# First FFN's rows by token halves, products ahead of lower parts, later turns, last attention values inside a projection

## The chip, the cores and the metric

One core of a Trainium2 chip runs the whole program. The metric is the device time of one execution in microseconds, the median of several runs. Engines are named as in the profile: PE is TensorE (matmul), PEld its weight loads, DVE is VectorE, ACT is ScalarE, POOL is GpSimd, SP is SyncE, whose queue issues the weight loads from HBM.

## The reference: what is computed

Batch 1, 256 tokens, width 1024, everything in float32. Three layers in a row, each a mixer and a SwiGLU FFN of inner width 2816:

```python
# layer 1 (adaLN: shift, scale, gate come from c)
h = rms_norm(x, norm1_w) * (1 + scale1) + shift1
x = x + gate1 * (concat[gated_delta_rule(h), sliding_window_attention(h)] @ w_out)
h2 = rms_norm(x, norm2_w) * (1 + scale2) + shift2
x = x + gate2 * ((silu(h2 @ w_gate) * (h2 @ w_up)) @ w_down)
# layer 2: short convolution mixer, then FFN
x = x + short_conv_mixer(rms_norm(x, mix_norm[0]));  x = x + swiglu(rms_norm(x, ffn_norm[0]))
# layer 3: dilated attention (3 branches, 16 heads), then FFN
x = x + dilated_attention_mixer(rms_norm(x, mix_norm[1]));  x = x + swiglu(rms_norm(x, ffn_norm[1]))
return rms_norm(x, final_norm)
```

## The kernel before

**Split arithmetic.** Each float32 factor is split into a high part (rounded to the matmul format, fp32r, by a ScalarE copy) and a low part (VectorE: the value less its high part). Each product is three matmuls: high x high, high x low, low x high. Weights come as blocks of 128 x 2048 floats (1 MB) through a ring of three buffers `raw`. For each block SP issues the load when the low part of the block three loads earlier is done (`load`), ScalarE makes `w_hi` (`hi(w)`, L663), VectorE `w_lo` (`lo(w)`, L1049). Both engines go through hand-written queues, strictly in order. `lo_ready`, `block_used` and so on are semaphores; PE's `block_used` tells ScalarE when a weight slot is free.

**An FFN** (`ffn(f)`, f = 0, 1, 2 in each engine's part) has 11 steps j. For each j PE makes gate and up of 256 inner features for token half t = 0 and t = 1 (`gate_up(f, j, t)`, 24 matmuls of 512 columns each into bank B[t]; lhs is the activation, 128 tokens of it). ScalarE takes silu of the gate half (`silu`, L901), VectorE multiplies it with the up half (`product(f, j, t)`, L1512 for f = 0, L1509 else) into `hid`. `turn_hid` turns `hid` with four PE transposes (L2254); ScalarE copies the high part (L906), VectorE makes the low part (L1517). `token_rows` multiplies it with the down block of the step before, in four pieces (feature half c, token half t) of six matmuls each, and `turn_hid(f, j)` stands in the middle of it (`halfway`). For f = 0 and j = 2 to 5 VectorE also has an `accumulate` (L1071 to L1075), two instructions of 1024 columns that build gate2.

**The norm ahead of the first FFN** (norm 1, x kept by features: 8 tiles k of 128 features x 256 tokens). PE spreads the root over the partitions (`rstd`), VectorE scales tile k (L1121), ScalarE makes its high part with the shift added (`h_high`, L688), VectorE the low part (L1126); VectorE's order is scaled(0), scaled(1), low(0), scaled(2), low(1), ... Each is one instruction of 256 columns. `gate_up(0, 0, 0)` waits for the low part of each k. Behind `h_high(1)` ScalarE has the `w_hi` of block 1's gate and up, an activation table load and `silu(0, 0, 0)`; behind `h_parts_2` VectorE has the two `w_lo` and `product(0, 0, 0)`. `gate_up(0, 1, 0)` waits for both `w_lo` and for that product.

**Norms 2 to 5** (x kept by tokens in `xt`) begin inside the last `token_rows` of the layer before. VectorE adds each finished piece to `xt` (`add_piece`, L1480; two instructions, L1477 and L1478, for norm 2). Ahead of the fourth piece (`before_last`) PE turns the first feature half of `xt` (`turn(n, 0)`, 8 transposes, L1769), ScalarE makes the high parts (L925) and squares the pieces (L917), VectorE the low parts (`low(k)`, L1487). PE's next block uses them at once; `turn(n, 1)` comes after its first two k (three for norm 2). VectorE puts the fourth addition behind three low parts for norm 2 and behind four for the others (`ahead`).

**The last attention pair** (a = 5): PE has `scores`, two blocks of the output projection (`ATT_OUT`, `ATT_OUT + 1`), `transposes` (L2033), then `values` (24 small matmuls), which wait for ScalarE's copies of the turned probabilities (L815), and then the blocks `ATT_OUT + 2` and `+ 3`. ScalarE's copies stand behind two `w_hi` of the next FFN. `ATT_OUT + 3` waits for the low part of those values (`pv_lo`).

Of the kernel before, what the change touches and what calls it, by code (L numbers as in the profile page):

```python
# [9 lines left out]
P = 128  # L10
T = 256
TT = T // P
HALF = P // 2
D = 1024
KD = D // P
# [152 lines left out]
class Semaphores:  # L168


    def __init__(self, new):
# [50 lines left out]
        self.t_ready = new("t_ready")  # L222
        self.h_hi_ready = new("h_hi_ready")
# [92 lines left out]
def build(nc, stream, x_in, consts_in, vectors_in, gab_in, t5_onehot, t5_log, rel_bias, out):  # L316
    t5_scratch = nc.dram_tensor("t5_scratch", (16, 384), F32, kind="Internal")
    with ExitStack() as ctx:
# [323 lines left out]
        def _(act):  # L642
# [41 lines left out]
            def h_high(n, ks=range(KD)):  # L684
                for k in ks:
                    act.wait_ge(s.t_ready, 8 * n + k + 1)
                    if n:
                        act.activation(normed(n)[0][:, k, :], nt[:, k, :], ACT.Identity, bias=shift2[:, k:k + 1]).then_inc(s.h_hi_ready, 1)  # L688
                    else:
                        act.activation(normed(n)[0][:, k, :], nt[:, k, :], ACT.Copy).then_inc(s.h_hi_ready, 1)  # L690
# [241 lines left out]
            def ffn(f, following):  # L932
# [3 lines left out]
                else:  # L936
                    squares(1)
                    root(1)
                    h_high(1)
# [98 lines left out]
        def _(dve):  # L1038
# [76 lines left out]
            def h_parts_2():  # L1115
                dve.wait_ge(s.rstd_ready, 2)
                dve.wait_ge(s.mod_ready, 6)
                rstd = B[3][:, 256:512]

                def scaled(k):  # L1120
                    dve.scalar_tensor_tensor(out=nt[:, k, :], in0=x[:, k, :], scalar=a2[:, k:k + 1],  # L1121
                                             in1=rstd, op0=ALU.mult, op1=ALU.mult).then_inc(s.t_ready, 1)

                def low(k):
                    dve.wait_ge(s.h_hi_ready, 8 + k + 1)
                    dve.scalar_tensor_tensor(out=normed(1)[1][:, k, :], in0=nt[:, k, :], scalar=shift2[:, k:k + 1],  # L1126
                                             in1=normed(1)[0][:, k, :], op0=ALU.add, op1=ALU.subtract).then_inc(s.h_lo_ready, 1)

                for k in range(KD):
                    scaled(k)  # L1130
                    if k >= 1:
                        low(k - 1)
                low(KD - 1)
# [348 lines left out]
            def turn(n, last):  # L1482
# [9 lines left out]
                ahead = 3 if n == 2 else 4  # L1492
# [27 lines left out]
            def ffn(f, following):  # L1520
# [6 lines left out]
                for j in range(JF):  # L1527
# [9 lines left out]
                    if j == 1:  # L1537
                        hid_low(f, 0)
                    if 0 < j < JF - 1:
# [3 lines left out]
                    product(f, j, 1)  # L1543
# [123 lines left out]
        def _(pe):  # L1667
# [75 lines left out]
            def token_rows(w, oh_, ol_, k0, banks, order=BY_FEATURES, first=False, r=None, halfway=None, before_last=None):  # L1743
# [758 lines left out]
```

## Time and profile before

| | us |
|---|---|
| median of 3 runs (1001.93, 1002.17, 1003.58) | 1002.17 |
| the profiled execution | 1002.46 |
| its span, first to last instruction | 1000.7 |

| engine | busy us | share |
|---|---|---|
| PE | 972.4 | 97% |
| PEld | 840.5 | 84% |
| DVE | 611.5 | 61% |
| ACT | 476.4 | 48% |
| POOL | 36.8 | 4% |

The profile is of one execution. A row of the timeline is one instruction, or several of the same kind in a row (x4) with their common length; instructions of one engine overlap in their records, so an engine's pace is read from start to start. What stands in brackets is the idle time ahead of the row and the instruction that ended it.

### The profile page before, as it was taken

Reading aid. Unit: us, or ns where it says so; the run is one execution under the profiler, and the core shown is the slowest. Engines: PE = TensorE matmul, PEld = TensorE weight load, DVE = VectorE, ACT = ScalarE, POOL = GpSimd, SP = SyncE. Lnnn points to the kernel's source line nnn. Section 1 sums busy time; section 2 is a strip of 40 time slices with the busy share of each in tenths; the row PEclk is TensorE's granted clock in tenths of the full one; section 3 lists DMA queues with packets and bytes.
Section 4 is the critical chain, followed back from the end, with each engine's and each line's share of the span. In section 5 each row is a group of like instructions: output and inputs, shape, how many; then the busy total and the mean of one; then the engine's idle time right before and its main releaser. Section 6 shows DMA issues by size and latency. Waiting matters only on the chain.

```text
span 1000.7 us, 15257 instructions
## 1 busy us (share of the span) xinstructions
PE 972.4 (97%) x6523; PEld 840.5 (84%) x6523; DVE 611.5 (61%) x751; ACT 476.4 (48%) x635; POOL 36.8 (4%) x37
## 2 busy tenths in 40 slices
PE   5899999999999999999999999999999999999998
PEld 3699988988878888899888888888999888888886
DVE  2478998865656444777764545456776654545444
ACT  3376358446334344634363535355645563535343
POOL 0000542000000000000000000000000000000000
PEclk9799999999999999999999999999999999999999
DMA  9746422866675536364635454544643425464621
GB/s 344 292 155 226 169 86 86 295 236 228 237 267 206 215 131 230 132 224 163 235 115 202 165 214 159 220 151 151 246 167 129 150 103 211 158 220 151 227 85 42
DMA packets 31554, 185.66 MB, mean 186 GB/s; under 512 B 3008, under 2 KB 5504, under 8 KB 10752
## 3 DMA queue, kind: packets, MB, share of 16 engines
q1 hardware_dynamic: 29952, 180.37, 49.9%
q0 software_dynamic: 832, 3.17, 1.0%
q8 instruction: 51, 0.84, 0.3%
q10 hardware_dynamic: 704, 1.17, 0.3%
q14 instruction: 15, 0.12, 0.0%
HBM read 183.62 MB, written 1.07 MB: 185 GB/s over the span
## 4 chain that ended last, share of the span: by engine, by line
PE 80%; DVE 9%; DMA 4%; ACT 4%; issue 2%; POOL 0%; SPq 0%; DVEq 0%; ACTq 0%
PE bank L1669 43%; PE acc L1669 34%; ACT w_hi L663 2%; DVE w_lo L1049 2%; DMA raw<-stream 2%; DMA keys_queries<-stream 2%; PE bank L2254 2%; DVE XT L1210 1%; DMA AT<-stream 1%; DVE soft L1361 1%; DVE keys_queries L1066 0%; DVE XT L1341 0%; PE bank L2033 0%; DVE h_parts L1487 0%; PE bank L1769 0%
## 5 line engine op out<-in xcount | busy, mean ns | idle before, releaser
L1049 DVE TENSOR_TENSOR w_lo<-raw,w_hi 128x2048 fp32r<-128x2048 f32 x145 | 329.3, 2289 | 156.0 <-ACT w_hi L663 155.6
L1669 PE MATMUL bank<-w_hi,h_parts 128*128 128x512 f32 x1056 | 333.5, 391 | 1.3 <-DVE h_parts L1126 1.3
L663 ACT ACTIVATE w_hi<-raw 128x2048 fp32r<-128x2048 f32 x145 | 273.0, 1907 | 100.4 <-PE acc L1669 71.2
L1669 PEld LDWEIGHTS bank<-w_hi,h_parts 128*128 128x128 f32 x1056 | 198.2, 188 | 44.4 <-issue 2.1
L1669 PE MATMUL bank<-w_lo,h_parts 128*128 128x512 f32 x528 | 205.5, 389 | 0.0
L1669 PE MATMUL acc<-h_parts,w_hi 128*128 128x256 f32 x928 | 172.8, 288 | 3.5 <-DVE h_parts L1101 2.5
L1669 PEld LDWEIGHTS acc<-h_parts,w_hi 128*128 128x128 f32 x928 | 145.1, 192 | 7.1 <-issue 5.3
L1669 PE MATMUL acc<-h_parts,w_lo 128*128 128x256 f32 x464 | 132.3, 285 | 0.0
L1669 PE MATMUL acc<-w_hi,o_hi 128*128 128x512 f32 x296 | 118.9, 402 | 0.0
L1669 PEld LDWEIGHTS bank<-w_lo,h_parts 128*128 128x128 f32 x528 | 99.2, 188 | 19.9
L1669 PE MATMUL acc<-w_hi,o_lo 128*128 128x512 f32 x296 | 115.6, 391 | 0.0
L1669 PE MATMUL acc<-w_lo,o_hi 128*128 128x512 f32 x296 | 115.5, 390 | 0.0
L1669 PEld LDWEIGHTS acc<-h_parts,w_lo 128*128 128x128 f32 x464 | 89.2, 192 | 0.0
L1517 DVE TENSOR_TENSOR o_lo<-bank,o_hi 128x512 fp32r<-128x512 f32 x33 | 22.8, 691 | 79.1 <-ACT o_hi L906 79.1
L901 ACT ACTIVATE silu_and_hid<-bank,rms 128x256 f32<-128x256 f32 x44 | 20.9, 475 | 105.2 <-PE bank L1669 105.2
L1669 PEld LDWEIGHTS acc<-w_hi,o_lo 128*128 128x128 f32 x296 | 55.6, 188 | 12.3
L1669 PEld LDWEIGHTS acc<-w_hi,o_hi 128*128 128x128 f32 x296 | 55.6, 188 | 10.9 <-issue 0.2
L1669 PEld LDWEIGHTS acc<-w_lo,o_hi 128*128 128x128 f32 x296 | 55.7, 188 | 10.6
L906 ACT ACTIVATE o_hi<-bank 128x512 fp32r<-128x512 f32 x33 | 19.8, 599 | 77.4 <-PE bank L2254 77.3
L1509 DVE SCALAR_TENSOR_TENSOR silu_and_hid<-bank,rms,silu_and_hid 128x256 f32<-128x256 f32 x44 | 21.2, 481 | 36.8 <-ACT silu_and_hid L901 36.8
L1669 PE MATMUL bank<-h_parts,w_hi 128*128 128x256 f32 x192 | 34.7, 283 | 0.3 <-DVE h_parts L1487 0.3
L1669 PEld LDWEIGHTS bank<-h_parts,w_hi 128*128 128x128 f32 x192 | 29.4, 188 | 0.7 <-DVE h_parts L1487 0.5
(370 smaller groups left out, 973.2 us busy)
## 6 DMA issues: line engine op xcount, KB each, us to landing
raw<-stream SPq DMA_DIRECT2D x162, 1024.0 KB, 5.0
AT<-stream SPq DMA_DIRECT2D x2, 1024.0 KB, 12.0
qkT<-stream SPq DMA_DIRECT2D x2, 1024.0 KB, 11.8
X_inv<-stream SPq DMA_DIRECT2D x2, 1024.0 KB, 13.2
keys_queries<-stream SPq DMA_DIRECT2D x2, 1024.0 KB, 15.2
t_tables<-t_scratch POOLq DMA_DIRECT2D x1, 2048.0 KB, 10.8
x_res<-x_in SPq DMA_DIRECT2D x2, 512.0 KB, 5.3
t_tables<-t_scratch POOLq DMA_DIRECT2D x1, 1024.0 KB, 13.1
```

The lines of the kernel that those rows point to most:

```text
L663: act.activation(high_of(w), raw_of(r), ACT.Copy).then_inc(s.hi_ready, 1)
L901: act.activation(sg[:, T * t:T * t + T], B[t][:, 0:256], ACT.Silu, scale=rms[:, t:t + 1] if f else 1.0).then_inc(s.silu_ready, 1)
L906: act.activation(hid_parts(j)[0].rearrange("p a b -> p (a b)"), B[2][:, :], ACT.Copy).then_inc(s.hid_hi_ready, 1)
L1049: dve.tensor_tensor(low_of(w), raw_of(weight_load(w)), high_of(w), ALU.subtract).then_inc(s.lo_ready, 1)
L1210: ins = dve.scalar_tensor_tensor(out=o, in0=pad[:, mt, tap:tap + 256], scalar=vec[:, cw:cw + 1], in1=o, op0=ALU.mult, op1=ALU.add)
L1361: link(dve.tensor_reduce(st[:, 0, 2 * hh + part:2 * hh + part + 1], sc[:, hh, c0:c1], AX.X, ALU.max))
L1509: dve.scalar_tensor_tensor(out=o, in0=up, scalar=rms[:, t:t + 1], in1=gate, op0=ALU.mult, op1=ALU.mult).then_inc(s.hid_ready, 1)
L1517: dve.tensor_tensor(low.rearrange("p a b -> p (a b)"), B[2][:, :], high.rearrange("p a b -> p (a b)"), ALU.subtract).then_inc(s.hid_lo_rea ...
L1669: return pe.matmul(o, l, r, start=start, stop=stop, skip_group_check=True)
L2254: ins = pe.transpose(B[2][:, T * i + P * t:T * i + P * t + P], hid[:, T * t + P * i:T * t + P * i + P], ident)
```

## The change

There are four parts. In the first FFN's norm the scalings, high parts and low parts are made for token half 0 (all 8 k) and then for token half 1, with 128 columns each, and semaphores of their own for half 0 (`first_t`, `first_h_hi`, `first_h_lo`); `gate_up(0, 0, 0)` waits for half 0's low parts and `gate_up(0, 0, 1)` for half 1's. In the first FFN's steps 2 to 5 VectorE makes `product(f, j, 1)` ahead of the `w_lo` of the next up block and not behind it. The turn of a norm's first half moves from ahead of the last piece of `token_rows` to behind that piece's first three matmuls (`in_last` in place of `before_last`), for norms 2 to 5, and VectorE's fourth addition comes behind three low parts for all of them. The last `values` move from behind their transposes into the middle of `token_rows(ATT_OUT + 2)`.

```diff
@@ -220,6 +220,9 @@
         self.rms_ready = new("rms_ready")
         self.rstd_ready = new("rstd_ready")
         self.t_ready = new("t_ready")
+        self.first_t = new("first_t")
+        self.first_h_hi = new("first_h_hi")
+        self.first_h_lo = new("first_h_lo")
         self.h_hi_ready = new("h_hi_ready")
         self.h_lo_ready = new("h_lo_ready")
         self.gab_hi = new("gab_hi")
@@ -684,10 +687,14 @@
             def h_high(n, ks=range(KD)):
                 for k in ks:
                     act.wait_ge(s.t_ready, 8 * n + k + 1)
-                    if n:
-                        act.activation(normed(n)[0][:, k, :], nt[:, k, :], ACT.Identity, bias=shift2[:, k:k + 1]).then_inc(s.h_hi_ready, 1)
-                    else:
-                        act.activation(normed(n)[0][:, k, :], nt[:, k, :], ACT.Copy).then_inc(s.h_hi_ready, 1)
+                    act.activation(normed(n)[0][:, k, :], nt[:, k, :], ACT.Copy).then_inc(s.h_hi_ready, 1)
+
+            def h_high_tokens(t):
+                tok = slice(P * t, P * t + P)
+                ready, done = ((s.first_t, s.first_h_hi), (s.t_ready, s.h_hi_ready))[t]
+                for k in range(KD):
+                    act.wait_ge(ready, 8 * t + k + 1)
+                    act.activation(normed(1)[0][:, k, tok], nt[:, k, tok], ACT.Identity, bias=shift2[:, k:k + 1]).then_inc(done, 1)
 
 
             act.wait_ge(s.vectors_loaded, 16)
@@ -936,7 +943,8 @@
                 else:
                     squares(1)
                     root(1)
-                    h_high(1)
+                    h_high_tokens(0)
+                    h_high_tokens(1)
                 for j in range(JF):
                     if j:
                         hi(down_block(f, j - 1))
@@ -1113,24 +1121,28 @@
                 dve.wait_ge(s.mod_ready, 2 * half + 2)
 
             def h_parts_2():
+                dve.wait_ge(s.mod_ready, 6)
+
+                def scaled(k, t):
+                    tok = slice(P * t, P * t + P)
+                    dve.scalar_tensor_tensor(out=nt[:, k, tok], in0=x[:, k, tok], scalar=a2[:, k:k + 1],
+                                             in1=B[3][:, 256 + P * t:256 + P * t + P], op0=ALU.mult, op1=ALU.mult
+                                             ).then_inc(s.t_ready if t else s.first_t, 1)
+
+                def low(k, t):
+                    tok = slice(P * t, P * t + P)
+                    dve.wait_ge(s.h_hi_ready if t else s.first_h_hi, 8 * t + k + 1)
+                    dve.scalar_tensor_tensor(out=normed(1)[1][:, k, tok], in0=nt[:, k, tok], scalar=shift2[:, k:k + 1],
+                                             in1=normed(1)[0][:, k, tok], op0=ALU.add, op1=ALU.subtract
+                                             ).then_inc(s.h_lo_ready if t else s.first_h_lo, 1)
+
                 dve.wait_ge(s.rstd_ready, 2)
-                dve.wait_ge(s.mod_ready, 6)
-                rstd = B[3][:, 256:512]
-
-                def scaled(k):
-                    dve.scalar_tensor_tensor(out=nt[:, k, :], in0=x[:, k, :], scalar=a2[:, k:k + 1],
-                                             in1=rstd, op0=ALU.mult, op1=ALU.mult).then_inc(s.t_ready, 1)
-
-                def low(k):
-                    dve.wait_ge(s.h_hi_ready, 8 + k + 1)
-                    dve.scalar_tensor_tensor(out=normed(1)[1][:, k, :], in0=nt[:, k, :], scalar=shift2[:, k:k + 1],
-                                             in1=normed(1)[0][:, k, :], op0=ALU.add, op1=ALU.subtract).then_inc(s.h_lo_ready, 1)
-
-                for k in range(KD):
-                    scaled(k)
-                    if k >= 1:
-                        low(k - 1)
-                low(KD - 1)
+                for t in range(TT):
+                    for k in range(KD):
+                        scaled(k, t)
+                        if k >= 1:
+                            low(k - 1, t)
+                    low(KD - 1, t)
 
             def residual(last):
 
@@ -1489,7 +1501,7 @@
 
                 for i in range(3):
                     add_piece(n - 1, i, *BY_FEATURES[i], last)
-                ahead = 3 if n == 2 else 4
+                ahead = 3
                 for k in range(ahead):
                     low(k)
                 add_piece(n - 1, 3, *BY_FEATURES[3], last)
@@ -1536,11 +1548,15 @@
                     product(f, j, 0)
                     if j == 1:
                         hid_low(f, 0)
+                    late = f == 0 and j in (2, 3, 4, 5)
+                    if late:
+                        product(f, j, 1)
                     if 0 < j < JF - 1:
                         lo(gate_block(f, j + 1) + 1)
                     elif j and following:
                         lo(following)
-                    product(f, j, 1)
+                    if not late:
+                        product(f, j, 1)
                     if f == 0 and j == 7:
                         modulation(3)
                     if j:
@@ -1740,7 +1756,7 @@
                 if tiles[-1] == KD - 1:
                     ins.then_inc(s.block_used, 1)
 
-            def token_rows(w, oh_, ol_, k0, banks, order=BY_FEATURES, first=False, r=None, halfway=None, before_last=None):
+            def token_rows(w, oh_, ol_, k0, banks, order=BY_FEATURES, first=False, r=None, halfway=None, before_last=None, in_last=None):
 
 
                 pe.wait_ge(s.lo_ready, w + 1)
@@ -1757,6 +1773,8 @@
                         mm(bank, oh, wh, first and k == 0, False)
                         mm(bank, oh, wl, False, False)
                         ins = mm(bank, ol, wh, False, False)
+                        if i == 3 and k == 0 and in_last is not None:
+                            in_last()
                     if r is not None and i < 3:
                         ins.then_inc(s.acc_tile_done, 1)
                 ins.then_inc(s.block_used, 1)
@@ -2238,6 +2256,8 @@
                     if j + t == 0:
                         if k == 2 and after_two is not None:
                             after_two()
+                        pe.wait_ge(s.h_lo_ready if f else s.first_h_lo, 8 * n + k + 1 if f else k + 1)
+                    elif j + f == 0:
                         pe.wait_ge(s.h_lo_ready, 8 * n + k + 1)
                     mm(bank, high[:, k, tok], wh[:, k, :, :], k == 0, False)
                     mm(bank, high[:, k, tok], wl[:, k, :, :], False, False)
@@ -2300,7 +2320,7 @@
                     token_rows(down_block(f, j - 1), *hid_parts(j - 1), 0, A, first=j == 1, halfway=lambda: turn_hid(f, j))
                 pe.wait_ge(s.hid_lo_ready, JF * f + JF)
                 token_rows(down_block(f, JF - 1), *hid_parts(JF - 1), 0, A, order=BY_FEATURES if f < 2 else BY_TOKENS, r=2 * f + 1,
-                           before_last=(lambda: turn(2 * f + 2, 0)) if f < 2 else None)
+                           in_last=(lambda: turn(2 * f + 2, 0)) if f < 2 else None)
 
             ffn(0)
             for i in range(4):
@@ -2315,7 +2335,7 @@
                     pe.wait_ge(s.by_ready, 3)
                 pe.wait_ge(s.by_lo, i + 1)
                 token_rows(CONV_OUT + i, o_hi, o_lo, 2 * i, Bs, first=i == 0, r=2 if i == 3 else None,
-                           before_last=(lambda: turn(3, 0)) if i == 3 else None)
+                           in_last=(lambda: turn(3, 0)) if i == 3 else None)
             ffn(1)
             dil_q = lambda b: (lambda t: q2[:, b, t, :])
             dil_k = lambda b: (lambda t: k2[:, b, t, :])
@@ -2346,10 +2366,11 @@
                     token_rows(ATT_OUT + 1, o_hi, o_lo, 2, A)
                 if i:
                     transposes(a, Bs, sc2, const("flip"))
-                    values(a, Bs, pT2, dil_v(b), out=A[3] if i < 4 else Bs[0])
-            token_rows(ATT_OUT + 2, o_hi, o_lo, 4, A)
+                    if i < 4:
+                        values(a, Bs, pT2, dil_v(b), out=A[3])
+            token_rows(ATT_OUT + 2, o_hi, o_lo, 4, A, halfway=lambda: values(5, Bs, pT2, dil_v(1), out=Bs[0]))
             pe.wait_ge(s.pv_lo, 6)
-            token_rows(ATT_OUT + 3, o_hi, o_lo, 6, A, r=4, before_last=lambda: turn(5, 0))
+            token_rows(ATT_OUT + 3, o_hi, o_lo, 6, A, r=4, in_last=lambda: turn(5, 0))
             ffn(2)
             def turn_rows(c, t):
```

## Rows read from the trace of the kernel before

**Rows 1.** The page: busy time of each engine, and the weight loads to landing.

```profile
PE 972.4 (97%) x6523; PEld 840.5 (84%) x6523; DVE 611.5 (61%) x751; ACT 476.4 (48%) x635; POOL 36.8 (4%) x37
...
raw<-stream SPq DMA_DIRECT2D x162, 1024.0 KB, 5.0
```

**Rows 2.** Waits of PE: us in total, times, longest.

```profile
PE bank L2254 <- DVE silu_and_hid L1512: 1.1, 4, 0.3
...
PE bank L1769 <- DVE norm_tmp L1478: 0.3, 1, 0.3
...
PE bank L1669 <- DVE h_parts L1487: 0.3, 1, 0.3
```

**Rows 3.** Timeline of PE (start, length, instruction, idle before): first FFN's start, block 1's.

```profile
218.81 0.47 PE L1669 MATMUL bank<-w_hi,h_parts 128*128 128x512 f32 x1 [1.29 <-DVE h_parts L1126]
...
230.16 0.66 PE L1669 MATMUL bank<-w_hi,h_parts 128*128 128x512 f32 x2
```

**Rows 4.** Timeline of PE and ACT at the last attention values.

```profile
788.62 1.48 PE L2033 MATMUL bank<-consts,scores 128*128 128x128 f32 x12
790.83 1.90 PE L1669 MATMUL bank<-probsT,silu_and_hid 128*64 128x128 f32 x24 [0.73 <-ACT probsT L815]
...
790.22 1.59 ACT L815 ACTIVATE probsT<-bank 128x384 f32<-128x384 f32 x4
```

**Rows 5.** Timeline of PE around the hidden turn of step 5.

```profile
312.21 0.39 PE L1669 MATMUL acc<-w_hi,o_lo 128*128 128x512 f32 x1
...
312.89 0.39 PE L1669 MATMUL acc<-w_hi,o_lo 128*128 128x512 f32 x1
313.62 0.66 PE L2254 MATMUL bank<-consts,silu_and_hid 128*128 128x128 f32 x4 [0.33 <-DVE silu_and_hid L1512]
```

**Rows 6.** Timeline of PE at norm 3: turn, first use, second turn.

```profile
501.35 0.39 PE L1669 MATMUL bank<-w_hi,o_lo 128*128 128x512 f32 x1
501.59 1.03 PE L1769 MATMUL acc<-consts,norm_tmp 128*128 128x128 f32 x8
...
503.84 0.41 PE L1669 MATMUL bank<-w_hi,h_parts 128*128 128x512 f32 x1
...
505.47 1.09 PE L1769 MATMUL acc<-consts,norm_tmp 128*128 128x128 f32 x8
```

**Rows 7.** Timeline of DVE and ACT at the first FFN's start.

```profile
217.12 0.87 DVE L1121 SCALAR_TENSOR_TENSOR norm_tmp<-x_res,a,bank 128x256 f32<-128x256 f32 x2 [0.78 <-PE bank L1669]
218.18 0.48 DVE L1126 SCALAR_TENSOR_TENSOR h_parts<-norm_tmp,mods,h_parts 128x256 fp32r<-128x256 f32 x1 [0.19 <-ACT h_parts L688]
...
223.45 3.70 ACT L663 ACTIVATE w_hi<-raw 128x2048 fp32r<-128x2048 f32 x2
...
225.38 4.49 DVE L1049 TENSOR_TENSOR w_lo<-raw,w_hi 128x2048 fp32r<-128x2048 f32 x2 [1.32 <-ACT w_hi L663]
229.79 0.41 DVE L1512 TENSOR_TENSOR silu_and_hid<-silu_and_hid,bank 128x256 f32<-128x256 f32 x1
```

**Rows 8.** Groups by form, of DVE and ACT: count, busy us, mean ns, idle before.

```profile
L1361 DVE TENSOR_REDUCE soft<-scores 128x1 f32<-128x256 f32 x16 | 6.7, 420 | 0.6
...
L1361 DVE TENSOR_REDUCE soft<-scores 128x1 f32<-128x128 f32 x16 | 4.6, 286 | 0.5
...
L796 ACT ACTIVATE scores<-scores,soft 128x256 f32<-128x256 f32 x16 | 8.0, 497 | 13.7 <-DVE soft L1367 13.7
...
L796 ACT ACTIVATE scores<-scores,soft 128x128 f32<-128x128 f32 x16 | 6.2, 387 | 0.0
```

**Rows 9.** Timeline of ACT and DVE ahead of that turn.

```profile
310.81 0.36 ACT L901 ACTIVATE silu_and_hid<-bank 128x256 f32<-128x256 f32 x1
...
310.94 2.29 DVE L1049 TENSOR_TENSOR w_lo<-raw,w_hi 128x2048 fp32r<-128x2048 f32 x1 [1.86 <-ACT w_hi L663]
313.14 0.41 DVE L1512 TENSOR_TENSOR silu_and_hid<-silu_and_hid,bank 128x256 f32<-128x256 f32 x1
```

**Rows 10.** Timeline of DVE at norm 3: the low parts.

```profile
503.15 1.66 DVE L1487 SCALAR_TENSOR_TENSOR h_parts<-acc,vec,h_parts 128x256 fp32r<-128x256 f32 x4 [0.68 <-ACT h_parts L925]
```

## Prediction

> **What bounds the kernel now.** I read the page first. TensorE (PE) is busy 97% of the span [rows 1]: no stage is bound by another engine or by DMA for long, so a change can only close or open single gaps in PE's queue. Then the waits of PE, to see which gaps the change aims at. They are small: four waits of the hidden turn for the product (1.1 us), one of the turn for VectorE's addition (0.3), one for a low part behind it (0.3) [rows 2], one of 1.29 us at the start of the first FFN [rows 3] and one of 0.73 us at the last attention values [rows 4]. Last the timelines around each gap, where the reader should look at starts and not at idle time: PE's instructions overlap, so a gap costs what its start comes later than the usual step. That step is 0.227 us for a 512-column product (three of them from 312.21 to 312.89) [rows 5], and 0.23 from a product to a transpose (501.35 to 501.59) [rows 6].
>
> **Part 1, first FFN by token halves.** Removed: 8 scalings and 8 low parts of 256 columns on VectorE, 8 high parts on ScalarE. Added: twice as many of 128 columns; all of token half 0 goes first, then all of half 1. PE's first 24 products wait only for half 0.
>
> Cost of one: a 256-column instruction of this kind takes 0.48 us, and two in a row take 0.87, so one follows another after 0.39 [rows 7]. No such instruction of 128 columns is in the trace. The nearest rows of VectorE fall from 420 to 286 ns when the columns are halved, and those of ScalarE from 497 to 387 [rows 8]. I take these differences off: 0.35 us long and 0.26 us apart on VectorE. Between the end of the first scaling (217.60) and the start of the first low part (218.18) lie 0.58 us for the high part and two handovers [rows 7]; halved that is 0.47.
>
> The new pipeline: a scaling to its own low part takes 0.35 + 0.47 = 0.82, and the scaling of k + 2 starts 0.26 after the low part of k, so two of the eight k take 1.08 us, one takes 0.54 (PE uses one per 3 x 0.227 = 0.68, so PE is not held back inside a half). Starts: first low part 217.12 + 0.82 = 217.94, the eighth 217.94 + 7 x 0.54 = 221.72, half 1's first scaling 221.98, its first low part 222.80, its eighth 226.58. PE can start at 217.94 + 0.35 + 0.15 = 218.44 and not at 218.81 (0.15 is what passes between 218.66 and 218.81 now) [rows 3, 7], and it reaches half 1 at about 223.9, when that half's first low part is there.
>
> But the queues behind it move. ScalarE's two w_hi copies of the next gate and up blocks start at 223.45, right behind the last high part, and VectorE's two w_lo and the first product come behind them (225.38 and 229.79) [rows 7]. The last high part now ends just ahead of 226.58, where the same recurrence with 0.39 and 0.58 gives 223.6 for today: **2.95 us later**. All that stands behind it in both queues comes 2.95 us later: the product ends at 230.20 + 2.95 = 233.15, and block 1's gate and up products on PE wait for this product and for both low parts. Today the first of them starts at 230.39 (the second of the pair at 230.16) [rows 3], only 0.04 after 230.20 + 0.15: there is no slack. It will start at 233.3. What the earlier start at 218.44 and the unheld k's win (48 products take 11.57 us today against 48 x 0.227 = 10.9) is all spent waiting there. **Part 1: +2.9 us.** Bounds: were the cost exactly proportional to columns, the recurrence ends 0.35 us later, so +0.3; were the start-to-start time 0.29 and not 0.26, +3.4. I take +2.9, since both nearest pairs of rows show a fixed share. A gain is excluded as long as a half costs at least half.
>
> A rule of the Trainium skill speaks against this part, too. "VectorE: DVE Perf Modes", section "The TRN2 errata", says that each VectorE and ScalarE instruction pays a fixed latency, and advises tiles of 512 elements or more. Its figure for VectorE, 58 cycles at 0.96 GHz, would make 16 more instructions cost an estimated 1.0 us, and the whole change would then come out at about 1002.1. The rows of this trace give a larger fixed share (0.39 less the 0.27 that 256 columns take by the difference of 0.134 per 128 is 0.12 us), and I go by them.
>
> **Part 2, product ahead of the lower part (blocks 2 to 5).** VectorE has the second product behind a w_lo that ScalarE's w_hi let start at 310.94, although the silu it needs was done at 311.17 [rows 9]. The turn on PE starts 0.73 after the product ahead of it (312.89 to 313.62) where 0.23 is usual [rows 5, 6]: 0.49 us for this one, of which the view shows 0.33 as idle. By the same reckoning the four are 1.1 idle [rows 2] and 0.16 each that the overlap hides, 1.7 together. Afterwards the product runs 311.2 to 311.6, 1.5 us ahead of PE. Queued behind it: the w_lo starts at 311.5 and not at 310.94, ends 0.6 later, at 313.8. PE wants it with the next gate block, behind the turn and 12 more products, which, now without the wait, is at 313.1 + 0.4 + 2.7 = 316.2: still 2.4 us of cover. SyncE's load into the buffer which that w_lo frees is issued 0.6 later too; a load takes 5.0 us [rows 1], its copy comes ahead of VectorE's two accumulations and is needed by PE only a block later. I cost both at nothing; were that cover gone, 4 x 0.6 = 2.4 us would be lost. **Part 2: -1.7 us** (bounds -1.7 and +0.7).
>
> **Part 3, turns 3 products later, additions ahead of the fourth low part.** The turn of the next norm's first half moves behind three products, 3 x 0.227 = 0.68 us. For norm 3 it starts at 501.59 without any wait, and PE's first product with h_parts at 503.84 [rows 6] comes just 0.05 after the low part is there: that ends at 503.15 + 0.48 = 503.64, plus 0.15 [rows 10]. Turn, high parts and low parts are one chain without a gap, so that low part is ready at 504.47 and PE starts 0.63 later than 503.84. Part of it comes back: the second turn, at 505.47, waits 0.23 today for the fourth addition, which is now queued behind three low parts and not four and no longer late. It starts at 505.93, 0.46 later. Behind it ScalarE's squares are also 0.68 late and with them the next high and low parts, for another 0.05 (an estimate: these have about 0.1 more slack than PE's 0.46). **Norm 3: +0.5.** Norms 4 and 5 repeat this pattern within 0.1 us: +0.45 and +0.5. Norm 2 is the one whose turn waits, 0.34 us [rows 2], 0.50 by starts. It waits for the two-step addition, so it starts 0.18 later than now with three products done ahead of it; the low parts come 0.18 later as well, PE has nothing left to fill with, and the 0.50 becomes a wait at the block's start: +0.1. **Part 3: +1.55 us** (bounds: -0.5 if the chain has slack I do not see, +2.4 if all the 0.68 of three norms and 0.4 of norm 2 are lost).
>
> **Part 4, last values inside the projection.** PE waits behind twelve transposes, 0.11 apart from 788.62 on and so the last at 789.83, to 790.83: 1.00 from start to start [rows 4]; the copies end at 791.81, since two w_hi copies stand ahead of them. Now 12 products (2.8 us) fill that, and the values start at about 792.7 with all copies done. One more change between kinds of product costs a little (0.1 to 0.2 in the starts): 1.00 - 0.12 = **-0.9 us**. The high and low copies of the values then have 12 products, 2.7 us, where 1.5 are needed, so the next wait, for pv_lo, isn't late (bounds -0.9 and -0.7).
>
> **Sum.** +2.9 - 1.7 + 1.55 - 0.9 = +1.85 us. The profiled execution is 1002.46 with a span of 1000.7, 1.8 of it outside the span; it is 0.3 above the median 1002.17, and the three runs reach from 1001.93 to 1003.58. So the span should be 1002.5 and the median **1004.0**.
>
> **Rivals.**
> - *Half-width instructions are cheap.* Part 1 costs 0.3, the rest as above: 1002.17 + 0.3 - 1.7 + 1.55 - 0.9 = 1001.4, within 0.2%. Against it: the fixed share in both pairs of [rows 8].
> - *The intended result: the waits go and nothing is late next.* Part 1 wins 0.37 + 0.65, part 2 1.7, norm 2's turn 0.5, part 4 0.9: 1002.17 - 4.1 = 998.1, faster. For it: all four waits are real [rows 2, 3, 4, 5]. Against it: the product at 229.79 and the low part at 503.15 are already just in time.
> - *The norm chain loses all of the shift (slower).* If PE gets nothing back at the second turns, because the fourth addition or the squares are late there, part 3 costs 2.4: 1004.9. It decides from the point where part 3 costs over 1.7 us with part 1 at 2.9; a part 1 of over 3.1 does the same.
> - *Part 2 wins nothing*, because the low part that gives way is missed by the next block: 1002.17 + 2.9 + 0 + 1.55 - 0.9 = 1005.7. Against it: 2.4 us of cover.
>
> **How the numbers follow.** A difference of about 0.2% (2.0 us) is what the measurement tells from none, so the borders are 1000.2 and 1004.2. The forecast (1003.3 to 1004.8) has 0.60, and since its middle lies just inside the border, 0.36 of that is within 0.2% and 0.24 is slower. Cheap halves have 0.13 (same), the intended result 0.08 (faster), the full loss of the shift 0.14 and part 2 for nothing 0.05 (both slower). Same 0.49, slower 0.43, faster 0.08. The range, 1001.4 to 1005.2, reaches over the forecast, cheap halves and the full loss, and leaves out the intended result and part 2 for nothing.
>
> **What would show it.** Part 1: halves of some 0.35 us on VectorE, PE's first product near 218.4, the first w_hi behind them near 226.4, and a new PE wait of 3 to 4 us for the product near 233; no such wait, and I am wrong by up to 3 us. Part 2: no waits of the hidden turns in blocks 2 to 5. Part 3: a wait for h_parts of 0.4 to 0.6 us at the start of norms 3, 4 and 5, and none at the second turns. Part 4: no wait at the values. Wrong above all if ScalarE's two w_hi copies start earlier than I say.

## The result, and the profile after

| | before | after |
|---|---|---|
| median | 1002.43 us (15 runs, 1000.54 to 1003.67) | 1005.61 us (15 runs, 1003.33 to 1009.17) |
| profiled execution | 1002.46 | 1009.17 |
| its span | 1000.7 | 1007.3 |
| PE busy | 972.4 | 975.7 |

The changed kernel is slower: ratio 1.0033, 95% interval 1.0023 to 1.0044, so +3.3 us (2.3 to 4.4). The forecast was +1.85, and 1005.61 lies 0.4 above the top of the range. The cause in one line: each of the four parts cost or won about what the sum said (within 0.3 us), and besides TensorE's clock fell to half behind the new wait, which the sum had not priced (1.6 us).

The two profiled executions differ by 6.6 us of span, twice what the medians do. The reader should first see that half of this lies ahead of the change. These are the last transposes of x in norm 1 (the norm ahead of the first FFN), in the changed kernel; the last of the four starts 0.33 later, at 220.33. (Columns of a timeline: start, length, instruction, how many in a row, idle time ahead and what ended it.)

```profile
220.00 0.60 PE L2282 MATMUL acc<-consts,x_res 128*128 128x128 f32 x4
```

The same transpose starts at 217.25 before, and between 214.1 and 219.9 in the profiles of the experiments, though the work ahead of it is the same in nearly all. The cause is PE's granted clock, in stretches that no edit touches. Columns: stretch, its length, busy us and instructions of PE, PEld, DVE, ACT, POOL, then the granted PE clock, DMA share, GB/s. First the kernel before, then the changed one:

```profile
38.00:42.00 4.00, 3.96 (x23) 3.13 (x24) 0.12 (x1) 0.60 (x1) 0.00 (x0) 0.68 1.01 426
42.00:50.00 8.00, 8.00 (x53) 7.75 (x53) 5.59 (x12) 3.97 (x6) 0.00 (x0) 0.73 0.17 62
...
140.00:180.00 40.00, 36.92 (x612) 34.66 (x610) 33.91 (x63) 28.73 (x72) 12.14 (x11) 1.00 0.26 88
```

```profile
38.00:42.00 4.00, 3.96 (x20) 2.54 (x20) 0.00 (x0) 0.60 (x1) 0.00 (x0) 0.55 1.01 426
42.00:50.00 8.00, 8.00 (x44) 8.00 (x45) 5.36 (x10) 3.38 (x5) 0.00 (x0) 0.59 0.14 58
...
140.00:180.00 40.00, 36.88 (x595) 34.93 (x594) 33.12 (x65) 29.39 (x77) 13.58 (x12) 0.96 0.19 61
```

Clock lost after and not before: 4 x 0.13 + 8 x 0.14 + 40 x 0.04 = 3.2 us at full rate, about the 3.08 by which the transpose is late. In the two profiles where the clock stays full from 33 to 210 us (five additions; second early copy) it starts at 214.2 and 214.1. So I compare from this transpose on: to the start of the last PE instruction it is 778.83 us before and 782.42 after, **+3.59**, close to the ratio.

What PE waits for in the changed kernel (us in total, times, longest). Of the waits of [rows 2] the hidden turns' and norm 2's for the addition are gone; the third, 0.3 for a low part of norm 2, is still there, as one of the four in the second row:

```profile
PE bank L1685 <- DVE silu_and_hid L1524: 3.8, 1, 3.8
...
PE bank L1685 <- DVE h_parts L1499: 1.7, 4, 0.5
...
PE bank L1685 <- DVE h_parts L1135: 1.0, 1, 1.0
...
PE acc L1685 <- DVE h_parts L1499: 0.5, 1, 0.5
```

PE at the first FFN's start and at block 1, to compare with [rows 3]:

```profile
221.59 0.47 PE L1685 MATMUL bank<-w_hi,h_parts 128*128 128x512 f32 x1 [0.98 <-DVE h_parts L1135]
...
232.33 0.39 PE L1685 MATMUL bank<-w_hi,h_parts 128*128 128x512 f32 x1
236.48 0.77 PE L1685 MATMUL bank<-w_hi,h_parts 128*128 128x512 f32 x1 [3.76 <-DVE silu_and_hid L1524]
237.04 0.63 PE L1685 MATMUL bank<-w_lo,h_parts 128*128 128x512 f32 x1
237.47 1.05 PE L1685 MATMUL bank<-w_hi,h_parts 128*128 128x512 f32 x2
...
239.92 0.63 PE L1685 MATMUL bank<-w_hi,h_parts 128*128 128x512 f32 x2
240.39 0.39 PE L1685 MATMUL bank<-w_lo,h_parts 128*128 128x512 f32 x1
```

Behind the wait one product follows another after 0.43 us (237.04 to 237.47), from 239.92 on after 0.23 again. The granted clock of these stretches says why (columns as above). It is at its lower level, 1.2 and not 2.4 GHz, nearly all of the 3.60 us:

```profile
220.00:232.00 12.00, 11.02 (x52) 9.04 (x51) 9.51 (x33) 8.55 (x18) 0.31 (x2) 1.00 0.81 259
232.00:236.40 4.40, 0.72 (x4) 0.26 (x2) 4.33 (x3) 4.37 (x7) 0.00 (x0) 1.00 0.33 101
236.40:240.00 3.60, 3.52 (x9) 2.83 (x10) 1.39 (x2) 3.60 (x5) 0.00 (x0) 0.53 1.02 416
240.00:250.00 10.00, 10.00 (x48) 8.26 (x47) 6.93 (x5) 3.89 (x5) 0.00 (x0) 1.00 0.65 233
```

VectorE and ScalarE there, to compare with [rows 7]:

```profile
221.09 0.35 DVE L1135 SCALAR_TENSOR_TENSOR h_parts<-norm_tmp,mods,h_parts 128x128 fp32r<-128x128 f32 x1 [0.21 <-ACT h_parts L697]
221.36 0.34 DVE L1128 SCALAR_TENSOR_TENSOR norm_tmp<-x_res,a,bank 128x128 f32<-128x128 f32 x1
...
229.70 0.35 DVE L1135 SCALAR_TENSOR_TENSOR h_parts<-norm_tmp,mods,h_parts 128x128 fp32r<-128x128 f32 x1 [0.17 <-ACT h_parts L697]
231.51 4.49 DVE L1057 TENSOR_TENSOR w_lo<-raw,w_hi 128x2048 fp32r<-128x2048 f32 x2 [1.45 <-ACT w_hi L666]
235.92 0.42 DVE L1524 TENSOR_TENSOR silu_and_hid<-silu_and_hid,bank 128x256 f32<-128x256 f32 x1
...
229.57 3.70 ACT L666 ACTIVATE w_hi<-raw 128x2048 fp32r<-128x2048 f32 x2
```

The halves last 0.35 us and start 0.26 to 0.27 apart. The first and the last low part are 8.61 apart (221.09 to 229.70); the w_hi pair, the w_lo pair and the product stand behind them as before, and PE behind the product.

### The profile page after: what moved, and what is told of

It reads as the page before. It is cut to its first block, busy times and chain, and to the rows that moved or that the text cites. A ratio compares the mean times of both kernels' runs of the same rounds, so it can differ in the third digit from the quotient of the medians.

```text
span 1007.3 us, 15281 instructions
## 1 busy us (share of the span) xinstructions
PE 975.7 (97%) x6523; PEld 843.9 (84%) x6523; DVE 614.0 (61%) x767; ACT 479.1 (48%) x643; POOL 36.8 (4%) x37
## 4 chain that ended last, share of the span: by engine, by line
PE 86%; DVE 8%; DMA 2%; ACT 2%; issue 1%; POOL 0%; SPq 0%; DVEq 0%; ACTq 0%
PE bank L1685 47%; PE acc L1685 36%; DMA keys_queries<-stream 1%; DVE w_lo L1057 1%; PE bank L2274 1%; DVE XT L1222 1%; DMA AT<-stream 1%; ACT w_hi L666 1%; PE bank L2051 1%; DVE keys_queries L1074 0%; ACT h_parts L932 0%; DVE XT L1353 0%; DVE h_parts L1135 0%; DVE norm_tmp L1128 0%; DVE XT L1215 0%
```

## The experiments

Four intervals carry most verdicts: from the start of norm 1's last transpose to PE's first product of the FFN; to the start of block 1; how long block 1's first 24 products take, from the start of the first to the start of the last; and from the transpose to the last PE instruction.

| kernel | first product | block 1 | 24 products | last PE | median us | ratio (95%) |
|---|---|---|---|---|---|---|
| before | 1.56 | 13.14 | 5.28 | 778.83 | | |
| after | 1.26 | 16.15 | 6.88 | 782.42 | 1005.61 | 1.0033 (1.0023 to 1.0044) |
| part 1 alone | 1.26 | 16.14 | 6.82 | 783.47 | 1007.11 | 1.0050 (1.0032 to 1.0067) |
| parts 2, 3, 4 | 1.56 | 13.14 | 5.31 | 777.52 | 1000.28 | 0.9987 (0.9971 to 1.0002) |
| part 3 alone | 1.56 | 13.12 | 5.30 | 780.53 | 1003.40 | 1.0014 (1.0000 to 1.0027) |
| parts 2, 4 and the addition | 1.56 | 13.13 | 5.29 | 775.34 | 999.07 | 0.9970 (0.9956 to 0.9984) |
| after, wait filled | 1.26 | 16.15 | 5.33 | 780.81 | 1002.45 | 1.0016 (1.0000 to 1.0032) |
| before, 3 additions | 1.56 | 15.28 | 6.94 | 782.33 | 1004.73 | 1.0030 (1.0015 to 1.0046) |
| before, 5 additions | 1.56 | 16.73 | 6.92 | 783.91 | 1006.76 | 1.0053 (1.0033 to 1.0072) |
| after, copy early | 1.26 | 14.60 | 5.32 | 779.28 | 1001.89 | 0.9998 (0.9983 to 1.0012) |
| before, 3 additions, again (one run) | 1.56 | 15.28 | 6.92 | 782.72 | | |
| after, copy early, again (one run) | 1.26 | 14.61 | 6.91 | 780.95 | | |
| after, copy early, third (one run) | 1.26 | 14.61 | 5.31 | 779.20 | | |

A ratio is to runs of the kernel before that were taken beside the same kernels: their median is 1000.91 beside the rows of part 1 alone, of parts 2, 3, 4, of parts 2, 4 and the addition and of the filled wait, and 1002.32 beside the others; the changed kernel's ratio is to the 1002.43 of the first table. So medians of different rows are compared by their ratios. Every kernel here computes all of the output. My theory after the result: part 1 costs 3.0 us by the queue and 1.5 by the clock, the rest is as forecast. The rivals: the clock would have fallen there anyway, or costs nothing on the whole; the excess comes from part 3 or from part 2.

### Part 1 alone

The kernel before, with the norm's halves and their semaphores and nothing else of the change (the central lines of the edit):

```diff
-                for k in range(KD):
-                    scaled(k)
-                    if k >= 1:
-                        low(k - 1)
-                low(KD - 1)
+                for t in range(TT):
+                    for k in range(KD):
+                        scaled(k, t)
+                        if k >= 1:
+                            low(k - 1, t)
+                    low(KD - 1, t)
```

> Part 1 alone (first FFN's norm by token halves) on the kernel before. Theory A, queue and clock: the first product of block 1 waits about 3.8 us for VectorE's product, starts 3.0 us later than in the kernel before relative to the norm ahead of it, and PE then runs some 3.4 us at half its clock (8 products 0.43 us apart), which costs 1.5 us more: +4.5 us, ratio 1.0045. Theory B, queue alone (the half clock behind the wait in the changed kernel was chance, as it is in other places of a run): +3.0 us, ratio 1.003, products 0.227 apart behind the wait. Theory C, the loss sits in the turns and not here: below +1 us.

Measured: ratio 1.0050 and +4.64 us from the transpose on. 3.00 of it is there when block 1 starts, 1.54 more when its first 24 products are done. PE's timeline:

```profile
229.26 0.39 PE L1681 MATMUL bank<-w_hi,h_parts 128*128 128x512 f32 x1
233.40 0.76 PE L1681 MATMUL bank<-w_hi,h_parts 128*128 128x512 f32 x1 [3.75 <-DVE silu_and_hid L1524]
233.96 0.63 PE L1681 MATMUL bank<-w_lo,h_parts 128*128 128x512 f32 x1
```

Same wait, same half rate behind it. All the loss of the change, and more, is part 1's.

### Parts 2, 3 and 4 without part 1

> Parts 2, 3 and 4 without part 1. Theory A (part 1 costs 4.5, the others give 1.7, cost 1.6 and give 0.9): -1.0 us, ratio 0.9990, no PE wait over 0.6 us after 205 us from the start but for none at block 1. Theory C (part 1 is harmless and the turns cost most): about +3 us, ratio 1.003, as the changed kernel.

Measured: 0.9987, and -1.31 from the transpose on. With part 1 alone that makes +3.33, near the +3.59 of the whole: the parts hardly touch each other. The interval of the ratio just includes 1, so it is the trace that carries this one. Its clock stays full at block 1 (5.31 us for the 24 products), so the fall doesn't come in any case.

### The changed kernel with the wait filled

14 products of zeros into a bank that nothing reads, where PE would wait for the product:

```diff
                 gate_up(f, 0, 1)
+                if f == 0:
+                    warm(14, B[2][:, :])
                 for j in range(1, JF):
```

> The changed kernel with 14 products of zeros (512 columns each, into a free bank, some 3 us) on PE inside the wait ahead of block 1; nothing reads them. Theory A: the wait for VectorE's product stays where it is, the idle stretch shrinks to about 0.7 us, the granted clock behind it stays at the upper level, and the time is 1.5 us below the changed kernel: +1.9 against the kernel before, ratio 1.002. Theory B: no difference from the changed kernel, ratio 1.0033 or what it shows now. A rival inside A, that the extra products delay PE: then block 1 starts later than 6.1 us behind.

PE's timeline, from behind the first of the 14: the other 13 zero products in the first row, block 1 behind them:

```profile
227.54 3.11 PE L1685 MATMUL bank<-zero_r 128*128 128x512 f32 x13
231.19 0.47 PE L1685 MATMUL bank<-w_hi,h_parts 128*128 128x512 f32 x1 [0.54 <-DVE silu_and_hid L1524]
231.50 0.39 PE L1685 MATMUL bank<-w_lo,h_parts 128*128 128x512 f32 x1
231.72 0.63 PE L1685 MATMUL bank<-w_hi,h_parts 128*128 128x512 f32 x2
```

Block 1 starts as late as in the changed kernel (16.15), since nothing was done about VectorE's queue; but its 24 products take 5.33 and not 6.88, and the end comes 1.61 earlier. This separates the two costs of the wait: the time waited, and the clock afterwards. What is left, +1.98 from the transpose on, is my forecast of +1.85. The ratio, 1.0016 (+1.6 us), agrees, but its interval overlaps the changed kernel's, so it is the trace that separates the two. All executions point the same way, by the granted clock averaged over each: of the 26 executions of the kernels with a wait of over 3.4 us (after, part 1 alone, five additions) none is above 0.998, while 11 of 50 of the kernel before reach 1.000 and two of 12 with the wait filled 0.999.

### The wait without part 1

To see whether the clock's price belongs to a wait of any origin, the kernel before got linked additions (128 x 512, their result isn't read) on VectorE, between the two low parts ahead of the product; three of them, or five:

```diff
                         lo(gate_block(f, j + 1) if j < JF - 1 else down_block(f, j))
+                    if f + j == 0:
+                        for _ in range(3):
+                            link(dve.tensor_tensor(..., x[:, 0:2, :], x[:, 2:4, :], ALU.add))
```

> The kernel before, with three additions of 512 columns (0.72 us each with their handover, 2.2 us in all; nothing uses their result) in VectorE's queue between the two w_lo of block 1, so that the first product comes 2.2 us late and nothing else is changed. All theories: block 1 starts 2.1 us later on PE, whose idle stretch there is about 2 us. Theory A says more only with a longer wait: if 2 us of idle are enough for the clock to fall, +3.6 us (ratio 1.0036), else +2.1 (1.0021).

> The same with five additions, 3.6 us. PE idles about 3.4 us ahead of block 1, nearly as in the changed kernel, with the norm's instructions of full width. Theory A: +3.6 for the delay and +1.5 for 3.4 us at half clock behind it, +5.1 us, ratio 1.0051. Theory B, no clock price of an idle stretch: +3.6, ratio 1.0036, products 0.227 apart.

The timeline of the kernel with three:

```profile
231.35 0.39 PE L1672 MATMUL bank<-w_hi,h_parts 128*128 128x512 f32 x1
233.69 0.47 PE L1672 MATMUL bank<-w_hi,h_parts 128*128 128x512 f32 x1 [1.95 <-DVE silu_and_hid L1512]
...
234.22 0.62 PE L1672 MATMUL bank<-w_hi,h_parts 128*128 128x512 f32 x2
...
236.04 1.05 PE L1672 MATMUL bank<-w_hi,h_parts 128*128 128x512 f32 x2
```

Both pay the wait and the clock: +3.50 is 2.14 to block 1 and 1.66 in its 24 products, less 0.30 elsewhere; +5.08 with five is 3.59 and 1.64, less 0.15. With three the first products still run at full rate (two of them last 0.62) and only then the clock falls (1.05); the price is the same. The 0.30 and the 0.15 are gained at the hidden turns, whose waits vary by that much where part 2 is absent. So the clock's price does not grow with the wait: 1.95, 3.41 and 3.76 us idle all cost 1.5 to 1.7.

### A shorter wait by moving one copy

In the changed kernel, ScalarE's high part of block 1's gate weights went from behind the norm's halves to between the sixth and the seventh square of the norm:

```diff
                     act.activation(nt[:, m, :], x[:, m, :], ACT.Square).then_inc(s.squared, 1)
+                    if n and m == 5:
+                        hi(gate_block(0, 1))
...
-                    if f == 0 or j:
+                    if j:
                         hi(gate_block(f, j + 1) if j < JF - 1 else down_block(f, j))
```

> The changed kernel, with ScalarE's w_hi copy of block 1's gate weights moved from behind the high parts into the idle stretch between the sixth and seventh square (2.1 us free there). If it is the place of the copies behind 16 small instructions that costs part 1: VectorE's w_lo start right behind the last low part, the first product comes 1.5 us earlier than in the changed kernel, PE idles about 2.2 us ahead of block 1 in place of 3.8. With a clock that does not fall for that: 3.0 us below the changed kernel, about the time of the kernel before (ratio 1.000); if it falls: 1.5 below it, ratio 1.0018.

The product comes 1.55 earlier, PE is idle 2.18 and not 3.76, and the clock stayed full: 3.14 below the changed kernel, and level with the kernel before by the ratio (0.9998; +0.45 from the transpose on). But 2.18 is more than the 1.95 behind which it had fallen. Either the idle time doesn't decide, or not alone, so I repeated both.

> The kernel before with three linked additions on VectorE, once more; one profile. PE idle 1.9 to 2.0 us ahead of block 1 in either case. If the idle time alone decides the clock: half clock for 3.4 us again, the first 24 products of block 1 take 6.9 us, last norm turn to last PE instruction 782.3. If it also hangs on where the gap lies in time, which shifts from execution to execution: it may stay full, 5.3 and 780.8.

> The changed kernel with block 1's first high-part copy inside the squares, once more; one profile. PE idle 2.1 to 2.3 us ahead of block 1. If the idle time alone decides: full clock again, 5.3 us for the first 24 products, 779.3 to the last PE instruction. If it hangs on where the gap lies: it may fall, 6.9 and 780.9.

> The same kernel a third time, for another draw of where the gap lies: the idle time alone gives full clock (5.3 and 779.3) each time; the place of the gap gives a fall in some of the executions (6.9 and 780.9).

The two repeats of the early copy, on one chip (second run, then third):

```profile
228.72 0.47 PE L1687 MATMUL bank<-w_hi,h_parts 128*128 128x512 f32 x1 [2.19 <-DVE silu_and_hid L1526]
...
229.26 0.62 PE L1687 MATMUL bank<-w_hi,h_parts 128*128 128x512 f32 x2
...
229.94 0.83 PE L1687 MATMUL bank<-w_hi,h_parts 128*128 128x512 f32 x2
230.56 0.63 PE L1687 MATMUL bank<-w_lo,h_parts 128*128 128x512 f32 x1
```

```profile
233.12 0.47 PE L1687 MATMUL bank<-w_hi,h_parts 128*128 128x512 f32 x1 [2.18 <-DVE silu_and_hid L1526]
...
233.66 0.62 PE L1687 MATMUL bank<-w_hi,h_parts 128*128 128x512 f32 x2
...
234.79 0.39 PE L1687 MATMUL bank<-w_lo,h_parts 128*128 128x512 f32 x1
```

The same instructions with the same idle time: in one execution the clock fell (24 products in 6.91), in the other it didn't (5.31), and they end 1.75 apart. So for an idle time near 2 us the fall isn't decided by the kernel alone. What differs between executions is when the gap comes (its end is at 228.72 and 233.12 here). That this decides fits, but was not isolated. Over all profiles, at block 1 and at the FFN's start: it fell in three of three behind 3.4 us and more, in two of two behind 1.95, in one of three behind 2.18, and never behind 1.3, 1.0 or 0.5.

The longest wait alone doesn't decide elsewhere either. In the changed kernel the clock also fell at 157.8 us (0.51 from there to 161.3), where the waits ahead are 0.61, 0.97 and 0.51 us and PE is busy 2.46 of the 3.80 us before the fall. The kernel before has the same waits there and kept its clock; of the 13 profiles three show this fall (after; parts 2, 3, 4; three additions, again).

### Part 3 alone, and without its later turns

> Part 3 alone: turns three products later, and the fourth addition earlier. Theory A: waits for h_parts of 0.46 us at the start of all four norms, none at the turns: norm 2 +0.1 to 0.2, norms 3 to 5 +0.5 each: +1.6 us, ratio 1.0016. Rival, that the late turns are hidden: 0.5 us or less, and below 0 with what norm 2's turn wins.

Measured: +1.70 from the transpose on (ratio 1.0014, +1.4 us). PE's waits:

```profile
PE bank L1669 <- DVE h_parts L1487: 1.7, 4, 0.5
...
PE bank L2256 <- DVE silu_and_hid L1512: 1.3, 4, 0.5
...
PE acc L1669 <- DVE h_parts L1487: 0.5, 1, 0.5
```

Each of the four norms begins with a wait of 0.46 to 0.47: three are in the first row, norm 4's is the third. The other 0.3 of the first row is norm 2's, as before. The second row is the hidden turns, which without part 2 wait as before (1.1 there, 1.3 here: they vary by that much). By the starts of the same instructions 0.3 of the +1.70 arises there, and the norms cost +0.15, +0.40, +0.45 and +0.42, **1.4 together**.

The last kernel keeps parts 2 and 4 and of part 3 only `ahead = 3`, the fourth addition behind three low parts, with the turns where they were:

```diff
-                ahead = 3 if n == 2 else 4
+                ahead = 3
```

> Parts 2 and 4, and of part 3 only VectorE's earlier fourth addition (three low parts ahead of it), with the turns where they were. If the turn's move is what costs part 3 and the addition alone is good: hidden turns -1.7, values -0.9, second turns of norms 3 to 5 without their 0.23, 0.18 and 0.22 us: -3.2 us, ratio 0.9968. If the earlier addition only delays the fourth low part until PE misses it: -2.6 or less, with a wait for h_parts behind the second turns.

Measured: 0.9970 (0.9956 to 0.9984), 999.07 us, -3.49 from the transpose on; it **beats both kernels**. Norms 3 to 5 wait for nothing here, neither for h_parts nor for the fourth addition. By the starts of the same instructions they gain 0.28, 0.24 and 0.27, where 0.23, 0.18 and 0.22 were expected. Against parts 2, 3 and 4, which differ from it only in the later turns, it is 2.18 better by the traces (1.2 by the medians). Part 3 is thus two edits of opposite sign: the later turns cost about 2.2, and the addition's place wins 0.8, which leaves the 1.4 at the norms.

## Why the prediction was right or wrong

**Where it failed.** The step is "All that stands behind it in both queues comes 2.95 us later ... Part 1: +2.9 us". The delay was right and its effect on PE's start too. But the sum ended there: it took the products behind the new wait at their usual 0.227, though it named "a new PE wait of 3 to 4 us". They ran 0.427 apart until the clock came back, which makes the term +2.9 + 1.5 to 1.6 = +4.5, and part 1 alone measured +4.64. No rival held it and no bound of part 1 (up to +3.4, by the recurrence rather +3.5) did, so the top of the range was short by this term. The trace of before could have warned. Near 38 us PE waits for a load:

```profile
38.04 1.07 PE L1669 MATMUL bank<-keys_queries,c_columns 128*32 128x512 f32 x8 [1.78 <-DMA keys_queries<-stream]
```

(PE of the kernel before), and behind it stand the stretches with a granted clock of 0.68 and 0.73 that the section on the result shows. A wait of 1.78 us, half the size of the one I forecast, with half clock after it: that row was there to be priced, and I read the waits without the clock behind them. The page "TensorE: Matmul & The Clock Gate" of the Trainium skill says in its Part 1 that "the default state is throttled, and activity releases the throttle"; the trace agrees with the two levels (0.427 and 0.227 us a product). It was the rule to weigh against this change, and I weighed another.

**Part 1, the queue: right.** Forecast: PE starts 0.37 earlier, w_hi 2.95 later, the product 2.95 later, PE's block 1 at +2.9. Measured from the transpose on: 0.30 earlier, 3.04 later (229.57 - 220.33 against 6.20 before), 3.05 later, +3.01. The recurrence gave 8.64 from the first to the sixteenth low part, the rows show 8.61. The differences of [rows 8] carried over to another instruction: 0.35 long and 0.26 apart as taken. The Trainium skill's 58 cycles ("VectorE: DVE Perf Modes", "The TRN2 errata") would be 0.06 us of fixed cost. They hold for operands in SBUF, as the low parts have them; the scalings read a bank, for which the same row of the table has 120, 0.125 us. So by that page 16 more instructions are an estimated 1.5 us and not the 1.0 that the prediction gives. By the rows 128 columns cost 0.39 - 0.26 = 0.13 from start to start, which leaves 0.26 - 0.13 = 0.13 fixed. The rule's direction was right; the trace's price is above the page's mean of 0.09. *Cheap halves* and *the intended result* fall with this.

**Part 2: right.** By the steps ahead of the four turns (0.59, 0.68, 0.63 and 0.73 before, 0.23 after) it wins the 1.70 forecast; from block 1's products to behind the fourth turn it is 1.85. The reference itself varies: in the four kernels without part 2 the same stretch lies 0.3 below to 0.3 above the kernel before. The turn of step 5 follows its product after 0.23 and no wait (before: 0.73, [rows 5]):

```profile
319.25 0.39 PE L1685 MATMUL acc<-w_hi,o_lo 128*128 128x512 f32 x1
319.48 0.60 PE L2274 MATMUL bank<-consts,silu_and_hid 128*128 128x128 f32 x4
```

The later w_lo is missed by nobody. The rival *part 2 wins nothing* gave 1005.7, by accident the measured time: a right number by a wrong mechanism, since this wait is gone. A total alone would have confirmed it.

**Part 3: right.** Forecast +1.55; measured at the norms +1.4 alone and +1.8 in the changed kernel. At norm 3 PE waits for h_parts and gets a part back at the second turn, as the chain of [rows 6, 10] had it:

```profile
508.35 1.03 PE L1787 MATMUL acc<-consts,norm_tmp 128*128 128x128 f32 x8
...
509.69 0.40 PE L1685 MATMUL bank<-w_hi,o_lo 128*128 128x512 f32 x1
510.55 0.47 PE L1685 MATMUL bank<-w_hi,h_parts 128*128 128x512 f32 x1 [0.46 <-DVE h_parts L1499]
...
511.78 0.40 PE L1685 MATMUL bank<-w_hi,h_parts 128*128 128x512 f32 x1
512.01 1.04 PE L1787 MATMUL acc<-consts,norm_tmp 128*128 128x128 f32 x8
```

From 509.69 to 510.55 are 0.86, 0.63 more than a step, and the second turn follows without a wait. The first use is 6.71 later than the 503.84 of before and the second turn 6.54 later than 505.47: 0.17 comes back, where 0.17 was forecast (0.63 less 0.46). In this trace 0.2 is lost again a few products later, which part 3 alone doesn't show; 0.05 was forecast for it. *The norm chain loses all*, with its 2.4, falls with that.

**Part 4: right.** -0.98 between the same instructions, -0.9 forecast, and no wait is left at the values (compare [rows 4]):

```profile
799.64 0.39 PE L1685 MATMUL acc<-w_hi,o_lo 128*128 128x512 f32 x1
799.96 1.80 PE L1685 MATMUL bank<-probsT,silu_and_hid 128*64 128x128 f32 x24
```

**The sum, redone**, from the starts in the two traces: +3.01 (queue) + 1.60 (clock) - 1.85 (part 2) + 1.8 (part 3) - 0.98 (part 4) = +3.6; from the transpose on +3.59, by the ratio +3.3. That parts 2 and 3 were 0.15 to 0.25 off, to either side, is luck for the sum; the missing 1.6 is not made up by anything.

## What to carry to other kernels

A new wait of PE has two prices: what PE waits, and the products that follow at half clock. Where a change opens a gap of 2 us or more in PE's work, add up to the 1.6 us measured here as a term or, near 2 us, as a case with its own chance, or fill the gap with products nobody reads. At 157.8 us the clock fell behind several short waits close together, in three of 13 profiles; what decides there was not isolated either. Halving the instructions of a dependent chain is no pipelining for what stands behind the chain in the same in-order queues: it pays the fixed part of each (0.13 us here, for 16 more) and the filling of the chain a second time, 3 us in all, and the gain in front (0.3 us) was spent at the next wait. And of a part with several edits, take each alone: the two halves of part 3 had opposite signs, and the version with the better one (and without part 1) wins 3 us.

## What was not expected of the hardware

- The clock's fall costs the same, 1.5 to 1.7 us, behind 1.95 us of idle time as behind 3.76, and can come up to 1.5 us after PE has started again (228.72 in the second early copy, rate still full until about 230.2).
- The same kernel with the same 2.18 us of idle time had half clock in one of three executions: 1.75 us between executions that no edit made.
- By the same clock the start of the program varies by 6 us between profiled executions (214.1 to 220.33 for the same transpose), against 3.3 us for the whole effect. Two spans alone would have shown +6.6.
